# The second attention's twenty column projections: from three 256-column products per eighth to one of 256 and one of 512, with the result in two halves

## The chip, the cores and the metric

The kernel runs on one core of one Trainium2 chip. The metric is the device time of one launch in microseconds (us); the time before is the median of three runs. The engines are named as the profile names them: PE (TensorE's products), PEld (its weight loads), DVE (VectorE), ACT (ScalarE), POOL (GpSimd) and SP (SyncE, which issues most of the transfers).

## What is computed

256 tokens of width 1024 pass through two blocks. The first has a convolution, a gated delta rule, a pooling branch and a layer of 16384 experts. The second block, in which the change lies, is this:

```
h = rmsnorm(x, attn_norm)
proj = h @ w_in                       # 1024 -> 3*512 + 4*512
mq, mk, mv, rq, rk, rv, rg = split(proj)
moba_out = moba_attention(mq, mk, mv)           # 8 heads of 64, causal, ALiBi
ret      = retention_chunkwise(rq, rk, rv)      # 4 heads of 128
ret_out  = head_groupnorm(ret) * silu(rg)
x = x + concat(moba_out, ret_out) @ w_out
... convolved feed-forward layer, gated embedding, last norm
```

The column projections are mq and mk (eight tiles of 128 features, "QK2") and rq, rk, rg (twelve, "RET2"). mv and rv come just before, token by token, as eight weight tiles "V2".

## The kernel before

**Number format.** Every float32 factor is cut into a high and a low part in TensorE's reduced format. A product of x and w is then whi·xhi + whi·xlo + wlo·xhi. For the operand, both parts of an eighth (128 of the 1024 inputs) lie in one buffer, `parts`, of which `ahi` and `alo` are the two slices.

**Weights.** All weights come as tiles of 128x1024 from one array, in the order of their use, through four buffers. Per tile SP issues the transfer, ACT copies it to `whi` (`split_hi`, L454) and DVE subtracts for `wlo` (`split_lo`, L469). `hi_for(u)` and `lo_for(u)` make the tile three ahead of u (u + LEAD); they wait until the tile that had the buffer has been used (`w_used`). The order of the work is written out by hand: each engine has one program, runs it strictly in order, and meets the others at semaphores.

**Projection tiles.** `gemm_tile` (L481) makes 128 features by 256 tokens from one weight tile: eight eighths of three products of 256 columns, 24 products. `gemm_tile_wide` (L491), so far only in the feed-forward layer, needs two per eighth: wlo·xhi of 256 columns, and whi against both parts as one product of 512 columns. Its result lies in two halves of a PSUM bank that have still to be added. In the feed-forward layer ACT copies the upper half to `low` (`ff_low`, L1468) and DVE adds it to the lower one (L2075, L2085).

**Around the change.** PE makes the eight V2 tiles into four banks, then QK2 tile n into one of two banks (`late(4 + n % 2)`), from n = 2 on after result n - 2 has been taken away (`evac2`, L943). DVE takes a result away with one instruction, `scaled` (L1970): times the row of token scales, to `qk2` or `rgs`. After QK2, PE waits for all eight results and begins with `att_scores(0)`. The twelve RET2 tiles alternate between two banks in the same way (L1003), with the heads' attention between them: `att_scores` (waits for `s_max`, which DVE's `att_bias` gives), `att_transposed`, `att_out` (waits for `ao_sb`, which DVE's `att_evac` gives) and `ret_scores`. At the end PE waits for all twenty results (L1013) before the retention's products at L1018. DVE's step n of RET2 is att_bias(n + 1), lo_for, att_norm(n), scaled(n), then att_evac or ret_decay. ACT's program ahead of QK2 is the last `hi_for` of the V2 stretch (L1390), which waits for QK2 tile 0, then the four copies of V2's result to `vv` (L1396), a copy for the embedding (L1399), and the `hi_for` of QK2 (L1400).

Of the kernel before, what the change touches and what calls it, by code (L numbers as in the profile page):

```python
# [19 lines left out]
ALU = mybir.AluOpType  # L20
ACT = mybir.ActivationFunctionType
# [3 lines left out]
T = 256  # L25
# [36 lines left out]
W_QK2 = W_V2 + KT  # L62
N_QK2 = 8
W_RET2 = W_QK2 + N_QK2
N_RET2 = 12
# [6 lines left out]
RING = 4  # L72
# [28 lines left out]
def program(nc, x_tok, vecs, wts, c1, gate_w, rows, w_pool, keys, c2, ple_t, nrows, out):  # L101
    ctx = ExitStack()
    with ctx:
        s = {n: ctx.enter_context(nc.semaphore("s_" + n)) for n in SEMS}
# [5 lines left out]
        def place(name, shape, dt=F32, at=None):  # L110
            size = int(np.prod(shape)) * (2 if dt == F16 else 4)
            size = -(-size // 32) * 32
            if at is None:
                at, top[0] = top[0], top[0] + size
            else:
                at[0], at = at[0] + size, at[0]
            return nc.alloc_sbuf_tensor_at(name, [P] + list(shape), dt, offset=at)
# [136 lines left out]
        qk2 = place("qk2", [16, T], at=a)  # L254
        rgs = place("rgs", [RH, T], at=a)
# [12 lines left out]
        r_row = place("r_row", [T], at=a)  # L268
# [11 lines left out]
        low = place("low", [2, T], at=a)  # L280
        su = place("su", [T], at=a)
        sg = place("sg", [T], at=a)
# [7 lines left out]
        def bank(b0, n, base=0):  # L290

            return flat[:, b0 * 512 + base:b0 * 512 + base + n]

        def late(b0, n, base=0):

            return bank((0, 1, 6, 7, 2, 3, 4, 5)[b0], n, base)
# [181 lines left out]
        def w_k(j, k):  # L478
            return whi[:, j, k * P:(k + 1) * P], wlo[:, j, k * P:(k + 1) * P]

        def gemm_tile(pe, j, dst, content=None):  # L481


            for n in range(KT):
                if content is not None and n % 2 == 0:
                    pe.wait_ge(s["operand"], 4 * content + n // 2 + 1)
                k = 2 * QUARTERS[n // 2] + n % 2 if content == 1 else n
                m = products(dst, *w_k(j, k), ahi[:, k, :], alo[:, k, :], n == 0, n == KT - 1)
            m.then_inc(s["w_used"], 1)

        def gemm_tile_wide(pe, j, dst, content=None):  # L491

            for k in range(KT):
                if content is not None and k % 2 == 0:
                    pe.wait_ge(s["operand"], 4 * content + k // 2 + 1)
                wh, wl = w_k(j, k)
                nc.tensor.matmul(dst[:, 0:T], wl, ahi[:, k, :], start=k == 0, stop=False, skip_group_check=True)  # L497
                m = nc.tensor.matmul(dst, wh, parts[:, :, k, :], start=False, stop=k == KT - 1, skip_group_check=True)  # L498
            m.then_inc(s["w_used"], 1)
# [79 lines left out]
        def _(pe):  # L579
# [342 lines left out]
            for k in range(KT):  # L922
                u = W_V2 + k
# [16 lines left out]
            for n in range(N_QK2):  # L940
                pe.wait_ge(s["w_lo"], W_QK2 + n + 1)
                if n >= 2:
                    pe.wait_ge(s["evac2"], n - 1)  # L943
                gemm_tile(pe, n % RING, late(4 + n % 2, T))


            pe.wait_ge(s["evac2"], N_QK2)
# [51 lines left out]
            for n in range(N_RET2):  # L999
                if n % 2 and n + 1 < MH:  # L1000
                    att_scores((n + 1) // 2)
                pe.wait_ge(s["w_lo"], W_RET2 + n + 1)
                pe.wait_ge(s["evac2"], N_QK2 + n - 1)  # L1003
                gemm_tile(pe, n % RING, late(n % 2, T))
                if n % 2 == 0 and 2 <= n <= MH:
                    att_transposed(n // 2 - 1)
                if n % 2 and 3 <= n <= MH + 1:
                    att_out(n // 2 - 1)
                if n >= MH:
                    ret_scores(n - MH)  # L1010
# [60 lines left out]
            for f in range(FF):  # L1071
                u = W_FF + (3 * f - 1 if f else 0)
# [35 lines left out]
            for k in range(5):  # L1108
                u = W_PLEG + k
# [26 lines left out]
        def _(act):  # L1136
            A = nc.scalar.activation
# [29 lines left out]
            def hi_for(u):  # L1167

                split_hi(act, u + LEAD, (u + LEAD) % 4)
# [227 lines left out]
            m.then_inc(s["v_sb"], 1)  # L1397
            act.wait_ge(s["ple_in"], 16)
            A(pthi[:, :, :], pt[:, :, :], ACT.Copy).then_inc(s["ple_hi"], 1)  # L1399
            for u in range(W_QK2 + 2, W_RET2):  # L1400
                hi_for(u)
            def att_pt(h):
                act.wait_ge(s["pt_ps"], h + 1)
                if h >= 2:
# [3 lines left out]
            def att_exp(h):  # L1408
                act.wait_ge(s["s_max"], h + 1)
                if h >= 4:  # L1410
                    act.wait_ge(s["pt_ps"], h - 3)
                A(pr[:, h % 4, 0:P], sS[:, h % 2, 0:P], ACT.Exp, bias=mx[:, h, 2:3], scale=MD ** -0.5,
                  accum_out=sums[:, h, 0:1])
                A(pr[:, h % 4, P:3 * P], sS[:, h % 2, P:3 * P], ACT.Exp, bias=mx[:, h, 3:4], scale=MD ** -0.5,
                  accum_out=sums[:, h, 1:2]).then_inc(s["s_exp"], 1)

            for n in range(N_RET2):
                u = W_RET2 + n
                hi_for(u)
                if n < MH:  # L1420
                    att_exp(n)
                if n >= 8:
                    act.wait_ge(s["evac2"], N_QK2 + n + 1)
                    A(rgs[:, n - 8, :], rgs[:, n - 8, :], ACT.Silu).then_inc(s["rg_done"], 1)
                if n % 2 == 0 and 2 <= n <= MH:
                    att_pt(n - 2)
                    att_pt(n - 1)
# [47 lines left out]
            for f in range(FF):  # L1475
                u = W_FF + (3 * f - 1 if f else 0)
# [65 lines left out]
        def _(dve):  # L1542
            V = nc.vector
            ch = Chain(dve, s["dve_step"])
# [33 lines left out]
            def lo_for(u):  # L1578
                split_lo(dve, u + LEAD, (u + LEAD) % 4)
# [387 lines left out]
            dve.wait_ge(s["r_bc"], 1)  # L1967
            ch(V.tensor_copy(r_row[:, :], late(7, T)))

            def scaled(u, b0, dst):  # L1970

                dve.wait_ge(s["w_used"], u + 1)
                V.tensor_tensor(dst, late(b0, T), r_row[:, :], ALU.mult).then_inc(s["evac2"], 1)

            for n in range(N_QK2):
                lo_for(W_QK2 + n)
                scaled(W_QK2 + n, 4 + n % 2, qk2[:, n, :])
            dve.wait_ge(s["ple_hi"], 1)
            V.tensor_tensor(ptlo[:, :, :], pt[:, :, :], pthi[:, :, :].bitcast(F32), ALU.subtract).then_inc(s["ple_op"], 1)
            dve.wait_ge(s["c2_in"], 16)  # L1980
# [30 lines left out]
            for n in range(N_RET2):  # L2011
                if n + 1 < MH:
                    att_bias(n + 1)
                lo_for(W_RET2 + n)
                if n < MH:
                    att_norm(n)
                scaled(W_RET2 + n, n % 2, qk2[:, 8 + n, :] if n < 8 else rgs[:, n - 8, :])
                if n % 2 == 0 and 4 <= n <= MH + 2:
                    att_evac(n - 4)
                    att_evac(n - 3)  # L2020
                if n > MH:
                    ret_decay(n - MH - 1)
# [43 lines left out]
            for f in range(FF):  # L2066
                u = W_FF + (3 * f - 1 if f else 0)
                v = f % 2
                lo_for(u)
                dve.wait_ge(s["w_used"], u + 1)  # L2070
                if f >= 2:
                    dve.wait_ge(s["ff_gelu"], f - 1)
                up = su[:, :]
                dve.wait_ge(s["ff_low"], 2 * f + 1)
                V.tensor_tensor(up, late(v, T), low[:, 0, :], ALU.add).then_inc(s["ff_sum"], 1)  # L2075
                dve.wait_ge(s["ff_sum"], 2 * f + 1)
                ch(V.tensor_scalar(fu[:, v, :], up, vcol("conv2", 2 * FF + f), vcol("conv2_b", f), ALU.mult, ALU.add))
                ch(V.scalar_tensor_tensor(fu[:, v, 1:T], up[:, 0:T - 1], vcol("conv2", FF + f), fu[:, v, 1:T],
                                          ALU.mult, ALU.add))
                V.scalar_tensor_tensor(fu[:, v, 2:T], up[:, 0:T - 2], vcol("conv2", f), fu[:, v, 2:T],  # L2080
                                       ALU.mult, ALU.add).then_inc(s["ff_conv"], 1)
                lo_for(u + 1)
                dve.wait_ge(s["w_used"], u + 2)
                dve.wait_ge(s["ff_low"], 2 * f + 2)
                V.tensor_tensor(sg[:, :], late(2 + v, T), low[:, 1, :], ALU.add).then_inc(s["ff_sum"], 1)  # L2085
                dve.wait_ge(s["ff_sum"], 2 * f + 2)
                dve.wait_ge(s["ff_gelu"], f + 1)
                if f >= 2:
                    dve.wait_ge(s["ff_split"], f - 1)
                V.tensor_tensor(pf[:, v, :], fg[:, v, :], sg[:, :], ALU.mult).then_inc(s["ff_mul"], 1)  # L2090
                if f:
                    lo_for(u + 2)
                dve.wait_ge(s["ff_hi"], f + 1)
                V.tensor_tensor(plo[:, v, :], pf[:, v, :], phi[:, v, :].bitcast(F32), ALU.subtract)\
                 .then_inc(s["ff_split"], 1)
# [150 lines left out]
```

## Time and profile before

| | |
|---|---|
| median of three runs | 1301.79 us (1301.33 to 1303.52) |
| the profiled execution | 1304.9 us, of which the span of instructions is 1303.1 us |
| PE busy | 1282.0 us, 98% |
| DVE, ACT busy | 962.9 us (74%), 760.4 us (58%) |
| granted TensorE clock, mean | 0.995 of full speed |

The busy time of PE is the time in which at least one product is recorded as under way. Matmul ends are modelled and products overlap in the records, so the time that a product takes in a stream is the distance from its start to the start of the next one. Times in a timeline are from the start of the span. Brackets at the end of a line give the idle time of the engine before it and what ended that.

### The profile page before, as it was taken

The page shows a single profiled execution, that of the slowest core. Times are in us where ns is not written, and L with a number is a line of the kernel's source. Part 1 is how long each engine was busy: PE and PEld are TensorE (multiplying, and loading weights), DVE is VectorE, ACT ScalarE, POOL GpSimd, SP SyncE. Part 2 cuts the span into 40 slices and gives each one's busy share as a digit, 9 for nine tenths or more (in the row PEclk, how much of TensorE's full clock was granted, in tenths as well). Part 3 has the DMA queues.
Part 4 walks back from the last instruction along what each step waited for, and adds up shares of the span by engine and source line. Part 5 has one row for each costly group of instructions (what it writes and reads, how often), then busy time and mean ns, then how long its engine had stood idle before and what let it go on. Part 6 is the DMA issues. An engine that isn't in the chain of part 4 may idle for free. (4 is left out here: it accounts for less than half of the span.)

```text
span 1303.1 us, 25968 instructions
## 1 busy us (share of the span) xinstructions
PE 1282.0 (98%) x8501; PEld 1165.4 (89%) x8501; DVE 962.9 (74%) x1898; ACT 760.4 (58%) x1153; POOL 484.0 (37%) x276
## 2 busy tenths in 40 slices
PE   8999999999999999998999999999999999999997
PEld 8999899999999999997888888888889988888886
DVE  6886677999899468874666666666666768777775
ACT  6833556777777766654555555555565557555556
POOL 1010001888887888787777674000000000000000
PEclk9999999999999999998999999999999999999999
DMA  7459654767676766667888888777774335555551
GB/s 259 150 179 386 214 178 145 190 182 180 176 193 179 193 178 162 161 161 168 216 216 218 218 215 250 236 240 241 227 247 166 131 131 170 188 190 187 186 193 65
DMA packets 119324, 253.00 MB, mean 194 GB/s; under 512 B 44336, under 2 KB 60848, under 8 KB 118752
## 3 DMA queue, kind: packets, MB, share of 16 engines
q1 hardware_dynamic: 77232, 229.24, 53.9%
q0 software_dynamic: 42032, 22.99, 11.2%
q8 instruction: 33, 0.54, 0.2%
q14 instruction: 27, 0.22, 0.1%
HBM read 234.23 MB, written 17.96 MB: 194 GB/s over the span
## 5 line engine op out<-in xcount | busy, mean ns | idle before, releaser
L469 DVE TENSOR_TENSOR wlo<-raw,whi 128x1024 fp32r<-128x1024 f32 (+1 forms) x500 | 508.5, 1033 | 122.6 <-ACT whi L454 111.4
L454 ACT ACTIVATE whi<-raw 128x1024 fp32r<-128x1024 f32 x412 | 434.8, 1058 | 236.7 <-PE ps L476 225.5
L420 POOL DMA_INDIRECT gates_dense<-gate,spot x256 | 472.5, 1846 | 168.8 <-issue 77.8
L474 PE MATMUL ps<-parts,whi 128*128 128x256 f32 x1472 | 422.4, 287 | 2.1 <-DVE parts L561 1.9
L475 PE MATMUL ps<-parts,whi 128*128 128x256 f32 x1472 | 416.2, 283 | 0.0
L476 PE MATMUL ps<-parts,wlo 128*128 128x256 f32 x1472 | 416.2, 283 | 0.0
L474 PEld LDWEIGHTS ps<-parts,whi 128*128 128x128 f32 x1472 | 282.0, 192 | 4.6 <-issue 4.1
L475 PEld LDWEIGHTS ps<-parts,whi 128*128 128x128 f32 x1472 | 282.1, 192 | 0.0
L476 PEld LDWEIGHTS ps<-parts,wlo 128*128 128x128 f32 x1472 | 281.9, 191 | 0.0
L474 PE MATMUL ps<-whi,phi 128*128 128x512 f32 x600 | 235.3, 392 | 4.9 <-DVE plo L1904 4.3
L475 PE MATMUL ps<-wlo,phi 128*128 128x512 f32 x600 | 234.6, 391 | 0.0
L476 PE MATMUL ps<-whi,plo 128*128 128x512 f32 x600 | 234.5, 391 | 0.0
L474 PEld LDWEIGHTS ps<-whi,phi 128*128 128x128 f32 x600 | 113.3, 189 | 28.8 <-DVE plo L1904 3.8
L1904 DVE TENSOR_TENSOR plo<-ea,phi 128x256 fp32r<-128x256 f32 x128 | 55.1, 430 | 112.4 <-ACT phi L1328 103.4
L476 PEld LDWEIGHTS ps<-whi,plo 128*128 128x128 f32 x600 | 113.3, 189 | 23.9
L475 PEld LDWEIGHTS ps<-wlo,phi 128*128 128x128 f32 x600 | 113.3, 189 | 23.7
L498 PE MATMUL ps<-parts,whi 128*128 128x512 f32 x352 | 125.2, 398 | 0.0
L1317 ACT ACTIVATE ea<-ps 128x256 f32 x116 | 44.5, 384 | 96.6 <-PE ps L476 93.8
L497 PE MATMUL ps<-parts,wlo 128*128 128x256 f32 x352 | 99.1, 282 | 0.9 <-DVE parts L561 0.7
L498 PEld LDWEIGHTS ps<-parts,whi 128*128 128x128 f32 x352 | 66.1, 188 | 16.0
L497 PEld LDWEIGHTS ps<-parts,wlo 128*128 128x128 f32 x352 | 66.4, 189 | 2.5 <-issue 0.9
L438 POOL DMA_DIRECT2D wrow<-in_nrows x1 | 0.6, 580 | 146.7 <-DVE plo L1904 146.7
(373 smaller groups left out, 1320.6 us busy)
## 6 DMA issues: line engine op xcount, KB each, us to landing
raw<-in_wts SPq DMA_DIRECT2D x412, 512.0 KB, 3.9
gates_dense<-pf POOLq DMA_DIRECT2D x4, 4096.0 KB, 30.8
gd<-gates_dense SPq DMA_DIRECT2D x22, 256.0 KB, 5.0
gd<-gates_dense SPq DMA_DIRECT2D x10, 512.0 KB, 6.1
gates_dense<-gate,spot POOLq DMA_INDIRECT x256
cst<-in_c POOLq DMA_DIRECT2D x1, 1216.0 KB, 7.5
xt<-in_x_tok SPq DMA_DIRECT2D x2, 512.0 KB, 4.5
kk<-in_keys POOLq DMA_DIRECT2D x1, 1024.0 KB, 5.2
```

What stands on the lines that cost most here:

```text
L420: pl.indirect_dma_start(out=dense, out_offset=bass.IndirectOffsetOnAxis(ap=spot[:, tb, h, k:k + 1], axis=0), in_=gate[:, tb, h, k:k + 1], ...
L438: pl.dma_start(wrow[:, :, :].rearrange("p a n -> p (a n)"), nrows.partition_broadcast(P)).then_inc(s["nrows_in"], 16)
L454: nc.scalar.activation(whi[:, j, :], raw_tile(j // 2, j % 2), ACT.Copy).then_inc(s["w_hi"], 1)
L469: m = nc.vector.tensor_tensor(wlo[:, j, c], raw_tile(j // 2, j % 2)[:, c], whi[:, j, c].bitcast(F32), ALU.subtract)
L474: nc.tensor.matmul(out_ap, wh, xh, start=first, stop=False, skip_group_check=True)
L475: nc.tensor.matmul(out_ap, wh, xl, start=False, stop=False, skip_group_check=True)
L476: return nc.tensor.matmul(out_ap, wl, xh, start=False, stop=last, skip_group_check=True)
L497: nc.tensor.matmul(dst[:, 0:T], wl, ahi[:, k, :], start=k == 0, stop=False, skip_group_check=True)
L498: m = nc.tensor.matmul(dst, wh, parts[:, :, k, :], start=False, stop=k == KT - 1, skip_group_check=True)
L1317: A(row_of(quad * 4 + n), late(n if four else n % 2, T), ACT.Gelu).then_inc(s["gelu"], 1)
L1904: V.tensor_tensor(plo[:, n % 2, :], row_of(oct_ * 8 + n), phi[:, n % 2, :].bitcast(F32), ALU.subtract)\
```

## The change

All twenty tiles use the wide form into a whole bank. ACT copies the upper half of each result to `low`, which the attention stretch shares with the feed-forward layer. DVE adds the lower half to that copy into `su` or `sg`, waits for the add, and then multiplies by the row of scales as before. ACT's copy of tile n stands in its program after the `hi_for` of step n (in RET2 also after `att_exp(n)`); for QK2 it stands behind the copies to `vv` and for the embedding. The semaphore `ff_low` counts from 20 when the feed-forward layer begins.

```diff
@@ PE, QK2 and RET2
-                gemm_tile(pe, n % RING, late(4 + n % 2, T))
+                gemm_tile_wide(pe, n % RING, late(4 + n % 2, 2 * T))
...
-                gemm_tile(pe, n % RING, late(n % 2, T))
+                gemm_tile_wide(pe, n % RING, late(n % 2, 2 * T))
@@ ACT
             A(pthi[:, :, :], pt[:, :, :], ACT.Copy).then_inc(s["ple_hi"], 1)
-            for u in range(W_QK2 + 2, W_RET2):
-                hi_for(u)
+            def low_half(t, b0):
+                act.wait_ge(s["w_used"], W_QK2 + t + 1)
+                if t >= 2:
+                    act.wait_ge(s["evac2"], t - 1)
+                A(low[:, t % 2, :], late(b0, T, base=T), ACT.Copy).then_inc(s["ff_low"], 1)
+            for n in range(N_QK2):
+                if n >= 2:
+                    hi_for(W_QK2 + n)
+                low_half(n, 4 + n % 2)
...
                 if n < MH:
                     att_exp(n)
+                low_half(N_QK2 + n, n % 2)
@@ DVE
-            def scaled(u, b0, dst):
-                dve.wait_ge(s["w_used"], u + 1)
-                V.tensor_tensor(dst, late(b0, T), r_row[:, :], ALU.mult).then_inc(s["evac2"], 1)
+            def scaled(t, b0, dst):
+                dve.wait_ge(s["ff_low"], t + 1)
+                both = (su, sg)[t % 2][:, :]
+                ch(V.tensor_tensor(both, late(b0, T), low[:, t % 2, :], ALU.add))
+                V.tensor_tensor(dst, both, r_row[:, :], ALU.mult).then_inc(s["evac2"], 1)
...
-                dve.wait_ge(s["ff_low"], 2 * f + 1)
+                dve.wait_ge(s["ff_low"], N_QK2 + N_RET2 + 2 * f + 1)
...
-                dve.wait_ge(s["ff_low"], 2 * f + 2)
+                dve.wait_ge(s["ff_low"], N_QK2 + N_RET2 + 2 * f + 2)
```

## Rows read from the trace of the kernel before

**Rows 1.** Busy time by stretch: stretch, its length, then engines, clock, DMA.
```profile
975.00:999.00 24.00, 23.48 (x196) 23.24 (x194) 13.26 (x17) 11.72 (x14) 0.00 (x0) 1.00 0.54 179
999.00:1047.00 48.00, 48.00 (x410) 44.72 (x411) 38.59 (x92) 26.10 (x58) 0.00 (x0) 1.00 0.40 132
...
1003.00:1027.00 24.00, 24.00 (x210) 22.06 (x210) 22.70 (x62) 13.14 (x35) 0.00 (x0) 1.00 0.41 134
```
**Rows 2.** Timeline of PE (start, us): first products of QK2 tiles 0, 2, 7.
```profile
975.20 0.28 PE L474 MATMUL ps<-parts,whi 128*128 128x256 f32 x1
...
980.95 0.28 PE L474 MATMUL ps<-parts,whi 128*128 128x256 f32 x1
...
995.35 0.28 PE L474 MATMUL ps<-parts,whi 128*128 128x256 f32 x1
```
**Rows 3.** Timeline of PE: two wide feed-forward tiles and what follows them.
```profile
1104.23 0.28 PE L497 MATMUL ps<-parts,wlo 128*128 128x256 f32 x1
...
1107.06 0.28 PE L497 MATMUL ps<-parts,wlo 128*128 128x256 f32 x1
...
1109.88 0.40 PE L474 MATMUL ps<-whi,phi 128*128 128x512 f32 x1
```
**Rows 4.** Timeline of DVE: results of QK2 tiles 0 and 7.
```profile
978.27 0.42 DVE L1973 TENSOR_TENSOR qk<-ps,r_row 128x256 f32<-128x256 f32 x1 [0.44 <-PE ps L476]
...
998.42 0.42 DVE L1973 TENSOR_TENSOR qk<-ps,r_row 128x256 f32<-128x256 f32 x1 [0.49 <-PE ps L476]
```
**Rows 5.** Timeline of PE: the first scores behind QK2, and scores 2.
```profile
998.90 0.49 PE L956 MATMUL ps<-qk 64*128 64x128 f32 x4 [0.52 <-DVE qk L1973]
...
1010.28 0.49 PE L956 MATMUL ps<-qk 64*128 64x128 f32 x4
```
**Rows 6.** Timeline of ACT: the feed-forward layer's copy of an upper half.
```profile
1107.26 0.39 ACT L1473 ACTIVATE low<-ps 128x256 f32<-128x256 f32 x1 [1.70 <-PE ps L498]
```
**Rows 7.** Timeline of DVE: the feed-forward layer's add and its next instruction.
```profile
1107.78 0.42 DVE L2075 TENSOR_TENSOR su<-ps,low 128x256 f32<-128x256 f32 x1 [0.96 <-ACT low L1473]
1108.24 0.41 DVE L2077 TENSOR_SCALAR fu<-su,words 128x256 f32<-128x256 f32 x1
```
**Rows 8.** Timeline of ACT from QK2's tile 0 on.
```profile
978.33 1.06 ACT L454 ACTIVATE whi<-raw 128x1024 fp32r<-128x1024 f32 x1 [1.81 <-PE ps L476]
979.29 2.40 ACT L1396 ACTIVATE vv<-ps,r_col 128x512 f32<-128x512 f32 x4
981.58 0.64 ACT L1399 ACTIVATE pthi<-pt 128x512 fp32r<-128x512 f32 x1
982.10 1.07 ACT L454 ACTIVATE whi<-raw 128x1024 fp32r<-128x1024 f32 x1
```
**Rows 9.** Timeline of DVE: end of bias 3, att_evac 2 and 3, last result.
```profile
1009.35 0.17 DVE L2004 TENSOR_SCALAR mx<-mx 128x2 f32<-128x2 f32 x1
...
1026.97 0.86 DVE L1993 COPY mix<-ps 64x256 f32<-64x256 f32 x2
...
1046.26 0.42 DVE L1973 TENSOR_TENSOR rgs<-ps,r_row 128x256 f32<-128x256 f32 x1 [0.44 <-PE ps L476]
```
**Rows 10.** Timeline of PE: att_out 2, and the retention's first products.
```profile
1030.05 0.44 PE L980 MATMUL ps<-pT,vv 128*64 128x128 f32 x4
...
1046.73 0.49 PE L1018 MATMUL ps<-vv,rS 128*128 128x128 f32 x2
```
**Rows 11.** Timeline of PE: two pauses elsewhere in the kernel.
```profile
8.06 1.95 PE L586 MATMUL ps<-ident,h 128*128 128x128 f32 x16 [1.76 <-ACT h L1156]
...
598.58 0.80 PE L474 MATMUL ps<-whi,phi 128*128 128x512 f32 x1 [3.57 <-DVE plo L1904]
```
**Rows 12.** Busy time by stretch behind the longer pause, and behind the shorter.
```profile
600.00:605.00 5.00, 5.00 (x14) 3.86 (x13) 1.61 (x4) 0.83 (x1) 4.26 (x3) 0.53 0.97 280
605.00:610.00 5.00, 5.00 (x24) 4.14 (x23) 3.16 (x7) 1.90 (x5) 4.21 (x3) 1.00 0.71 176
...
8.00:11.00 3.00, 2.85 (x24) 2.65 (x24) 2.68 (x6) 2.75 (x7) 0.00 (x0) 1.00 0.57 195
```

More of the change, by code:

```diff
@@ L1968, in _ @@
             ch(V.tensor_copy(r_row[:, :], late(7, T)))
-            def scaled(u, b0, dst):
-                dve.wait_ge(s["w_used"], u + 1)
-                V.tensor_tensor(dst, late(b0, T), r_row[:, :], ALU.mult).then_inc(s["evac2"], 1)
+            def scaled(t, b0, dst):
[3 more added lines that the diff above has]
+                V.tensor_tensor(dst, both, r_row[:, :], ALU.mult).then_inc(s["evac2"], 1)
             for n in range(N_QK2):
                 lo_for(W_QK2 + n)
-                scaled(W_QK2 + n, 4 + n % 2, qk2[:, n, :])
+                scaled(n, 4 + n % 2, qk2[:, n, :])
             dve.wait_ge(s["ple_hi"], 1)
@@ L2016, in _ @@
                     att_norm(n)
-                scaled(W_RET2 + n, n % 2, qk2[:, 8 + n, :] if n < 8 else rgs[:, n - 8, :])
+                scaled(N_QK2 + n, n % 2, qk2[:, 8 + n, :] if n < 8 else rgs[:, n - 8, :])
                 if n % 2 == 0 and 4 <= n <= MH + 2:
```

## The prediction

> **What bounds the kernel now.** I read the busy time by stretch first. From 975 us on, where the twenty tiles lie, PE is busy 23.48 of 24.00 us in QK2's stretch and 48.00 of 48.00 in RET2's, at the full granted clock (1.00, the 2.4 GHz level); ACT has about half its time free, DVE between 9 and 11 us in each [rows 1]. So PE is the bound, and only two things count: how long a tile takes on PE, and whether a later evacuation makes PE wait. In the second question an engine's mean load says little. From 1003 to 1027, in the middle of the attention, DVE is busy 22.70 of 24.00 us [rows 1]; it is no bound yet, but has nothing to give away. The timelines of the three engines then show each place at which PE meets ACT or DVE.
>
> **PE's tiles.** Seven narrow tiles lie between the starts at 975.20 and 995.35: 2.88 us each, 24 products at 0.120 [rows 2]. Two wide tiles in a row take 1104.23 to 1107.06 and 1107.06 to 1109.88, 2.825 us each with 16 products [rows 3]. A third fewer instructions thus save 0.054 us a tile, since the columns streamed are the same (6144); over 20 tiles that is -1.1 us, between -1.0 and -1.2 by the two wide tiles shown. Each of the eight products that go per tile is worth 7 ns.
>
> The Trainium skill, "TensorE: Matmul & The Clock Gate", section "Wait — 56ns, not 53.3ns?", gives a fixed cost of about 2.5 ns per product in a warm stream. By that the 160 products that go would be worth 0.4 us (an estimate from that page), and the sum below would end 0.7 us higher; the rows give almost three times as much per product, in this number format, and I go by the rows.
>
> **What an evacuation costs now and then.** Before, DVE's one multiply starts 0.2 us after the tile's end (978.27 against 975.20 + 2.88 = 978.08) and takes 0.42 [rows 2, 4]; PE starts 0.06 after its end (998.84 to 998.90) [rows 4, 5]. After, three steps stand in a row. The nearest rows are those of the same pair in the feed-forward layer: ACT's copy takes 0.39 (1107.26 to 1107.65) [rows 6], DVE's add begins 0.13 later at 1107.78, and the instruction chained to it 0.46 after that, at 1108.24 [rows 7]. So where PE waits for a result without cover, it waits 0.39 + 0.13 + 0.46 = 0.98 us longer. At least the two instructions' own 0.8 us is due; above, 1.1 if each hand-over costs 0.05 more.
>
> **The first tiles of QK2 (the largest term).** There are two banks, so tile 2 needs result 0. ACT's program reaches the copy of half 0 only behind the split that waits for tile 0 (978.33), the four copies to `vv` (979.29, 2.40 us) and the embedding's copy (981.58); its next instruction starts at 982.10 today [rows 8], and 0.05 earlier after, as tile 0 ends 0.05 earlier. From 982.05: copy to 982.44, add at 982.57, multiply 983.03 to 983.45, PE at 983.51. Wide tile 2 could start at 975.20 + 2 x 2.825 = 980.85. PE stands still for 2.7 us. Today the same result leaves at 978.27 [rows 4] and PE runs through (tile 2 at 980.95 [rows 2]): DVE did this alone, and ACT's 2.4 us of V2 copies cost nothing. Without hand-overs it would be 2.3, with DVE's late split in between 3.0. Behind the copy on ACT stand half 1 and the split of the sixth tile, some 0.6 us later than today; PE needs neither before it has done two more tiles, so one stall it is. From tile 3 on the chain of about 1.7 us (0.2 + 0.98 + 0.42 + 0.06) fits into the 2.83 that the other bank gives.
>
> **Behind QK2.** PE waits for all eight results before the first scores, and has nothing else to do: today 0.52 us idle [rows 5]. The full 0.98 comes on top: +1.0 (0.8 to 1.1).
>
> **In the attention.** DVE's add costs its queue 0.46 a tile and nothing leaves it. Two places feel it. First, scores 2 waits for bias 3, which ends at 1009.52 today, 0.70 (with the 0.06) ahead of PE's 1010.28 [rows 5, 9]; two adds make DVE 0.92 later and three wide tiles make PE 0.16 earlier: +0.4 (0.2 to 0.6). Second, att_out 2 waits for DVE's att_evac 2 and 3, done at 1027.83 today, 2.16 ahead of PE's 1030.05 [rows 9, 10]. Seven adds lie before it, 3.22 us; the stretch has 1.30 us idle at most to take them up [rows 1], and part of that is the short gaps of chained instructions, which can't be used. DVE is 1.9 to 3.2 later, PE about level (0.4 later by the first stall, 0.4 earlier by seven tiles): 0 to 1.1, and I take +0.4, as if some 0.6 us of the idle time were usable. ACT, free for nearly half of the time, hides its twenty copies (7.8 us) here: the split behind each copy needs the same tile's end anyway.
>
> **Behind RET2.** The retention's products start at 1046.73, just after the last result (1046.26 + 0.42 = 1046.68) [rows 9, 10]: no cover, +1.0 (0.8 to 1.1). What follows on DVE and ACT moves with PE. The feed-forward layer keeps its instructions, with another count in a wait.
>
> **The sum.** -1.1 + 2.7 + 1.0 + 0.4 + 0.4 + 1.0 = +4.4, with the unrounded terms (-1.07 + 2.66 + 0.98 + 0.38 + 0.40 + 0.98) +4.3 us. The profiled execution (1304.9 us, of which 1303.1 are span) would come to 1309.2 with a span of 1307.4. It lay 3.1 us above the median of the runs; the change does not touch what made that difference, so I add the sum to the median: 1301.8 + 4.3 = 1306.1 us. The low ends together give +2.9 (1304.7), the high ends +5.9 (1307.7).
>
> **Rivals.**
> 1. The front stall doesn't come, only the other terms: +1.6, 1303.4. It takes an ACT that reaches half 0 before 979.4 (980.85 less 0.06, 0.42, 0.46, 0.13 and 0.39). For it: the copy needs nothing that is late. Against it: ACT is strictly in its program's order there, without a gap between 978.33 and 982.10 [rows 8]. 10%.
> 2. Faster: PE's two banks hide every evacuation and its 1.1 us stay: 1300.7. It decides at the same point of ACT and, besides, wherever PE has less than the 0.98 us more of cover at both ends of the tiles. Against it: PE waits there already, 0.52 us before the first scores [rows 5]. 6%.
> 3. The wide form gives nothing beside the attention's small products: -1.1 falls away, +5.4, 1307.2. For it: 0.054 us of 2.88 is near what the rows resolve. Against it: all seven narrow tiles and both wide ones keep their pace [rows 2, 3]. 8%.
> 4. The clock falls in the front stall. After a pause of 3.57 us PE ran at the 1.2 GHz level [rows 11]: in the 5 us from 600 on at 0.53, 14 products of 512 columns instead of the 24 of the next 5 us [rows 12], so 10 x 5/24 = 2.1 us lost there and 0.7 in the 1.4 us before, 2.8 in all. After a pause of 1.76 us, early in the kernel, it read 1.00 [rows 11, 12]. Mine of some 2.5 us lies between. If it falls: +7.1, 1308.9. 12%. The Trainium skill, same page, section "A second HAM failure mode: psum-queue depth-cycling", says that many short idles between groups of products can bring the clock down too; the 0.52 us wait here did not (1.00 in that stretch), and no stall that I add is repeated.
>
> **How the numbers follow.** The forecast as worked out has 64%. The likeliest time is 1306.1. The range leaves out the faster case, most of the clock's case and a few per cent of the ends: 1303.2 to 1308.4. What a measurement of this kernel can tell from no change is about 0.2%, 2.6 us, so slower begins at 1304.4: the forecast (but for 2% at its low end), rivals 3 and 4, together 82%, of which I take 81; within 0.2%: rival 1, that low end and what I held back, 13%; faster 6%.
>
> **What would show it.** In the profile after: L497 and L498 in pairs every 0.353 us in QK2 and RET2; a pause of PE of about 2.4 to 2.7 us before QK2's tile 2, put down to DVE's multiply; ACT's first `low` at about 982, behind the embedding's copy; PE's wait before the first scores 1.5 instead of 0.5; DVE without idle time from 1006 to 1030; a wait of about 1 us before L1018; granted clock 1.00 throughout. The forecast is wrong if tile 2 starts with tile 1's end, if the wide tiles take 2.88 here, or if PE waits in most RET2 tiles for DVE, which would make DVE the bound of that stretch.

## The result and the profile after

The changed kernel takes 1307.26 us (median of 6 runs, 1306.35 to 1310.35) against 1302.50 us for the kernel before in the same job (6 runs, 1301.33 to 1303.52): ratio 1.0044, 95% interval 1.0033 to 1.0054. It is slower, by 4.8 us in the medians.

The profiled executions must be compared by stretch. Their spans are 1304.5 and 1303.1 us, only 1.4 apart, but QK2's tile 0 starts at 972.78 after and at 975.20 before [rows 2], ahead of anything that the change touches. From there to the start of L1025, where the output projection begins, it is 78.26 us after (to 1051.04) and 74.32 before (to 1049.52): **+3.94 us**. The rest, to the end of the span, is 253.5 and 253.6. All stretches below run between these two points.

The busy time by stretch after, in the same columns as [rows 1]; PE is no longer busy throughout, and DVE is busy 23.11 of 24.00 us in the attention:

```profile
975.00:999.00 24.00, 20.47 (x117) 17.51 (x115) 15.22 (x24) 13.04 (x21) 0.00 (x0) 1.00 0.47 159
999.00:1047.00 48.00, 46.62 (x310) 38.74 (x311) 42.37 (x102) 29.27 (x69) 0.00 (x0) 1.00 0.39 133
...
1004.00:1028.00 24.00, 23.57 (x160) 19.54 (x159) 23.11 (x63) 15.25 (x42) 0.00 (x0) 1.00 0.39 133
```

The timeline of ACT after, which answers to [rows 8]: the copies of halves 0 and 1 stand behind V2's four copies and the embedding's, without a gap.

```profile
975.86 1.06 ACT L454 ACTIVATE whi<-raw 128x1024 fp32r<-128x1024 f32 x1 [1.76 <-PE ps L498]
976.83 2.40 ACT L1396 ACTIVATE vv<-ps,r_col 128x512 f32<-128x512 f32 x4
979.10 0.64 ACT L1399 ACTIVATE pthi<-pt 128x512 fp32r<-128x512 f32 x1
979.62 0.67 ACT L1405 ACTIVATE low<-ps 128x256 f32<-128x256 f32 x2
```

The timeline of DVE after: it sat idle for 4.64 us until the half was there, then added and multiplied.

```profile
980.05 0.42 DVE L1984 TENSOR_TENSOR su<-ps,low 128x256 f32<-128x256 f32 x1 [4.64 <-ACT low L1405]
980.51 0.43 DVE L1985 TENSOR_TENSOR qk<-su,r_row 128x256 f32<-128x256 f32 x1
```

The timeline of PE after: the starts of tiles 0 and 1, then the five places where PE waited in the stretch (from 981.08 on, the lines with brackets), three of them with the start of what PE did before. Before, only the first scores had a wait, of 0.52 us [rows 5].

```profile
972.78 0.28 PE L497 MATMUL ps<-parts,wlo 128*128 128x256 f32 x1
...
975.60 0.28 PE L497 MATMUL ps<-parts,wlo 128*128 128x256 f32 x1
...
978.19 0.40 PE L498 MATMUL ps<-parts,whi 128*128 128x512 f32 x1
981.08 0.35 PE L497 MATMUL ps<-parts,wlo 128*128 128x256 f32 x1 [2.50 <-DVE qk L1985]
...
999.36 0.49 PE L956 MATMUL ps<-qk 64*128 64x128 f32 x4 [1.39 <-DVE qk L1985]
...
1009.72 0.82 PE L968 MATMUL ps<-ident,pr 128*128 128x128 f32 x6
1010.97 0.49 PE L956 MATMUL ps<-qk 64*128 64x128 f32 x4 [0.43 <-DVE mx L2016]
...
1027.34 0.36 PE L497 MATMUL ps<-parts,wlo 128*128 128x256 f32 x1
...
1030.94 0.44 PE L980 MATMUL ps<-pT,vv 128*64 128x128 f32 x4 [0.59 <-DVE mix L2005]
...
1047.12 0.39 PE L994 MATMUL ps<-qk 128*128 128x128 f32 x2
1048.25 0.49 PE L1018 MATMUL ps<-vv,rS 128*128 128x128 f32 x2 [0.75 <-DVE rgs L1985]
```

2.50 + 0.87 more than before + 0.43 + 0.59 + 0.75 = 5.14 us of waits. But a bracket counts from the modelled end of the product before it, and in a stream the next product starts ahead of that end: the last one of tile 1 starts at 978.19 and is drawn 0.40 us long, where such products follow each other after 0.23. So the brackets are somewhat short, and the five places are compared by starts here. The lines of the kernel before that answer to L968 and L994, and of run 3 (below) to 1027.34 and 1030.94:

```profile
1009.53 0.81 PE L968 MATMUL ps<-ident,pr 128*128 128x128 f32 x6
...
1046.48 0.38 PE L994 MATMUL ps<-qk 128*128 128x128 f32 x2
```
```profile
1021.48 0.36 PE L497 MATMUL ps<-parts,wlo 128*128 128x256 f32 x1
...
1024.43 0.44 PE L980 MATMUL ps<-pT,vv 128*64 128x128 f32 x4
```

Tile 2 starts 5.48 us after tile 1 instead of 2.825 [rows 3], 2.65 late. The first scores are 0.87 late (1.39 less 0.52). Scores 2 start 1.25 us after L968's first product instead of 0.75 (1010.28 [rows 5]), 0.50 late; att_out 2 starts 3.60 us after its tile instead of 2.95, 0.65 late; the retention's products start 1.13 us after L994 instead of 0.25 (1046.73 [rows 10]), 0.88 late. That is 5.55 us; the stretch grew by 3.94, so the products gave back 1.6.

### The profile page after: what moved, and what is told of

It is laid out like the page before. It is cut to its first block and busy times, and to the rows that moved or that the text cites. A ratio compares the mean times of both kernels' runs of the same rounds, so it can differ in the third digit from the quotient of the medians.

```text
span 1304.5 us, 25706 instructions
## 1 busy us (share of the span) xinstructions
PE 1279.7 (98%) x8341; PEld 1155.6 (89%) x8341; DVE 971.2 (74%) x1918; ACT 766.2 (59%) x1173; POOL 483.5 (37%) x276
## 5 line engine op out<-in xcount | busy, mean ns | idle before, releaser
L474 PE MATMUL ps<-parts,whi 128*128 128x256 f32 x1312 | 376.2, 287 | 1.9 <-DVE parts L561 1.8
L475 PE MATMUL ps<-parts,whi 128*128 128x256 f32 x1312 | 371.0, 283 | 0.0
L474 PEld LDWEIGHTS ps<-parts,whi 128*128 128x128 f32 x1312 | 251.4, 192 | 2.6 <-issue 2.2
L475 PEld LDWEIGHTS ps<-parts,whi 128*128 128x128 f32 x1312 | 251.5, 192 | 0.0
L498 PE MATMUL ps<-parts,whi 128*128 128x512 f32 x512 | 181.5, 396 | 0.0
L498 PEld LDWEIGHTS ps<-parts,whi 128*128 128x128 f32 x512 | 96.1, 188 | 22.3
L1483 ACT ACTIVATE low<-ps 128x256 f32<-128x256 f32 x44 | 16.9, 384 | 64.6 <-PE ps L498 64.5
```

Source lines behind the costliest of these rows:

```text
L474: nc.tensor.matmul(out_ap, wh, xh, start=first, stop=False, skip_group_check=True)
L475: nc.tensor.matmul(out_ap, wh, xl, start=False, stop=False, skip_group_check=True)
L1483: A(low[:, n, :], late(2 * n + f % 2, T, base=T), ACT.Copy).then_inc(s["ff_low"], 1)
```

## Experiments

The theory: all cost lies in the later evacuation of results, at five places, and the products themselves save about 1.1 us. The rivals: the products or the clock cost the time; or a wait that is taken away only moves to the next place. Line numbers are each kernel's own.

**1. The changed kernel again**, as a base.

> The changed kernel once more, as the base of this job. Theory (the late evacuations: 5.1 us of waits in the trace after, less 1.1 us that the products save): +4 to +5 us against the kernel before. Second question: two of its six runs so far lay 3 us above the others, with a lower mean clock (0.994 and 0.995 against 0.996 and 0.997). Rival for the part of the loss that the one trace does not hold: the 2.5 us pause ahead of QK2's tile 2 lets the clock fall in some executions. Then runs 3 us above the lowest show up here again and are gone in the run without that pause.

1305.05 us (1304.09 to 1306.18) against 1301.51 (22 runs, 1300.50 to 1302.99): ratio 1.0031, interval 1.0019 to 1.0043. The stretch is 78.23 us, with the same five waits (2.50, 1.39, 0.43, 0.54, 0.75). No run lies 3 us above the others here, so the two high ones of the first job did not come again; their cause stays open, as no trace shows them. The spread of 2 us is that of the kernel before; the last section shows a difference of this size that arises ahead of QK2.

**2. ACT's order at the front.** The definition of `low_half` moves ahead of the first line shown.

```diff
...
+            low_half(0, 4)
             act.wait_ge(s["w_used"], W_QK2)
             act.wait_ge(s["scale_ok"], 1)
             for b0 in range(4):
+                if b0 == 3:
+                    low_half(1, 5)
                 m = A(half_row(vv, b0), late(b0, 512), ACT.Copy, ...)
...
                 if n >= 2:
                     hi_for(W_QK2 + n)
-                low_half(n, 4 + n % 2)
+                    low_half(n, 4 + n % 2)
```

> ACT copies half 0 ahead of the four V2 copies and half 1 ahead of the last of them; nothing else differs from the changed kernel. Theory: the 2.5 us pause ahead of tile 2 goes, the other four waits stay: 2.5 us faster than the changed kernel, +1.5 to +2.3 against the kernel before. Rival A (DVE's longer queue is what counts, and the pause only moves): the waits at the first scores grow by what is gained, within 1 us of the changed kernel. Rival B (the clock falls in that pause in some executions): besides the 2.5 us, the spread between the lowest and the highest run shrinks from 4 us to about 2, as it was before the change.

1303.51 us (11 runs, 1301.79 to 1304.04): 1.0012, interval 1.0003 to 1.0021. The stretch falls to 75.83 us, 2.4 less than in run 1 on the same chip, and the other four waits stand as they were. PE's waits in this kernel (total, times, longest):

```profile
PE ps L956 <- DVE qk L1989: 1.4, 1, 1.4
PE ps L1018 <- DVE rgs L1989: 0.8, 1, 0.8
PE ps L980 <- DVE mix L2009: 0.6, 1, 0.6
PE ps L956 <- DVE mx L2020: 0.4, 1, 0.4
```

So the order of ACT's program makes the largest term. Rival A falls. Rival B is not borne out: the spread is 2.3 us with the pause gone, and was 2.1 in run 1.

**3. The products alone.** The kernel before with `gemm_tile_wide` at both places and nothing else; the upper half of each result is left out.

> The kernel before with the wide products alone: ACT copies nothing and DVE multiplies the lower half as before, so the products of the low part of the operand are left out of the result. Theory: all cost of the change is in taking the results away; this is 1.1 us faster than before (0.054 us a tile), and QK2's tiles start every 2.825 us without a pause. Rival (the wide form gives nothing here, or its stream is held up by the attention's products): no change or slower.

1299.24 us (11 runs, 1298.73 to 1301.46): 0.9986, interval 0.9977 to 0.9995. The stretch is 72.90 us, 1.42 less than before. PE has one wait left, the old one:

```profile
PE ps L956 <- DVE qk L1973: 0.5, 1, 0.5
```

QK2's tiles start 2.82 to 2.84 us apart instead of 2.88, as forecast; up to the first scores that is 0.41 us (23.70 to 23.29). RET2's gain more, 1.01 us or 0.08 a tile: from the start of its tile 1 to that of tile 2 it is 2.89 instead of 2.98, from tile 8 to tile 9 (with other products between) 4.11 instead of 4.21.

**4. The evacuation alone.** The changed kernel with `gemm_tile` at both places, and `late(b0, T)` in ACT's copy.

> The changed kernel with the narrow products of before; ACT copies the lower half instead of an upper one, so DVE's add doubles the result. Theory: it has all five waits and none of the saving: +5 us against before, 1.1 us slower than the changed kernel; the pause ahead of tile 2 is 0.1 us shorter, as two narrow tiles take 0.1 longer. Rival (the products cost the time, not the evacuation): near the kernel before.

1307.09 us (5 runs, 1305.70 to 1308.02): 1.0045, interval 1.0032 to 1.0059. The stretch is 80.46 us, +6.14, more than the +5 expected. The profile shows four waits (2.44, 0.87 more than before, 0.16 and 0.74) and none at att_out 2; by starts the five places are 2.60, 0.88, 0.23, 0.20 and 0.87 late, 4.8 us, less than in the changed kernel. The rest is the clock: the pause is no longer than in run 1, but behind it PE ran at the 1.2 GHz level for about three us. The busy time by stretch, with the clock in the last column but two:

```profile
977.00:979.00 2.00, 0.20 (x2) 0.00 (x0) 0.39 (x1) 2.00 (x6) 0.00 (x0) 1.00 0.04 14
979.00:982.00 3.00, 2.36 (x11) 2.39 (x12) 2.93 (x6) 0.80 (x1) 0.00 (x0) 0.51 0.08 18
982.00:985.00 3.00, 3.00 (x25) 3.00 (x25) 1.06 (x3) 0.95 (x2) 0.00 (x0) 0.92 0.82 287
```

Tile 2 takes 4.21 us here instead of 2.88: 1.33 us for the clock, and 4.8 + 1.3 = 6.1. In run 1 the same place reads 1.00:

```profile
976.00:979.00 3.00, 0.51 (x4) 0.21 (x2) 1.02 (x3) 3.00 (x6) 0.00 (x0) 1.00 0.11 45
979.00:982.00 3.00, 3.00 (x18) 2.67 (x19) 2.86 (x4) 0.14 (x1) 0.00 (x0) 1.00 0.25 86
```

**5 and 6. One stage at a time.** Tiles outside the set are narrow and are taken away by the old single multiply.

```diff
+        WIDE = (8, ..., 19)        # run 5: RET2's; run 6: (0, ..., 7), QK2's
...
+                if t not in WIDE:
+                    dve.wait_ge(s["w_used"], W_QK2 + t + 1)
+                    V.tensor_tensor(dst, late(b0, T), r_row[:, :], ALU.mult).then_inc(s["evac2"], 1)
+                    return
```

> Only RET2's twelve tiles are wide and taken away in halves; QK2's eight are as before. Theory (each wait belongs to its own tiles): the waits of the trace after at scores 2, att_out 2 and the retention's products stay (0.4 + 0.6 + 0.8), the two at QK2 go, the products give back 0.7 to 1.0: +0.8 to +1.1 us against before in the stretch. Rival (DVE's lag in the attention comes from what QK2 left behind): the attention's waits vanish too, and it is no slower than before.

RET2 alone: 1302.45 us (12 runs) against 1302.09 (32 runs), ratio 1.0003, interval 0.9994 to 1.0012. The stretch is 75.37 us, +1.05, with waits of 0.43, 0.58 and 0.75 and the old 0.52: as expected.

> Only QK2's eight tiles are wide; RET2 is as before. Theory: the pause of 2.5 us ahead of tile 2 and 0.9 more at the first scores, less 0.4 for the products: +2.9 us, and some 1.2 more where the clock falls in the pause, as it did in the trace of the run with the evacuation alone. With the RET2 part alone it adds up to the changed kernel's +4. Rival (the two parts hide each other): the two sums differ from the changed kernel by more than 1 us.

QK2 alone: 1306.97 us (9 runs, 1303.76 to 1308.18), ratio 1.0031, interval 1.0020 to 1.0043. The stretch is 78.64 us, +4.32, of which the clock is about 1.5 again: behind the pause of 2.50 us it is at 0.52, and tile 2 takes 4.31 us instead of 2.8.

```profile
978.00:981.00 3.00, 0.88 (x5) 0.50 (x3) 0.62 (x2) 3.00 (x7) 0.00 (x0) 1.00 0.24 90
981.00:984.00 3.00, 2.62 (x8) 2.34 (x9) 2.97 (x5) 0.54 (x1) 0.00 (x0) 0.52 0.17 40
```

Without it, 1.05 + 2.8 = 3.9 us: in the traces the two stages add up to the changed kernel's 3.94, and neither hides the other. The medians don't show that: QK2 alone is 4.9 us above the kernel before there, more than the whole change in run 1 (3.5). Its two quickest runs (1303.76 and 1304.49 us) have the highest mean clock, 0.998; the other seven have 0.995 or 0.996, in which the falls near 597 us (last section) count too.

**7. Front order, last tiles narrow.** Experiment 2 with tiles 7 and 19 narrow (`WIDE` = 0 to 6 and 8 to 18).

> ACT copies halves 0 and 1 ahead of the V2 copies, and the last tile of QK2 and of RET2 are narrow and taken away in one step, as before. Theory: only DVE's two waits in the attention are left (0.4 + 0.6) against 18 tiles' saving (1.3): -0.3 us against before, no measurable change. Rival (a wait that is filled moves to the next place): the first scores or the retention's products wait as long as in the changed kernel, +1.6 as without the front pause alone.

1302.57 us (12 runs, 1300.44 to 1305.45), ratio 1.0003, interval 0.9994 to 1.0013: no difference from before. The stretch is 74.53, +0.21 where -0.3 was expected; DVE's two waits are left (0.42, 0.54), and 0.21 before the retention's products. By starts the three places are 0.48, 0.60 and 0.35 late, 1.4 us, against the saving of 18 tiles (about 1.3): +0.1 of the +0.21. The forecast left out the last place: DVE's weight split behind tile 18's two instructions ends only at 1043.9, and the multiply of tile 19 follows it without idle time, where before DVE stood idle for 0.44 us ahead of it [rows 9].

**8. POOL multiplies.** As run 7; for RET2's tiles 0 to 7 DVE only adds.

```diff
+            for t in range(N_QK2, N_QK2 + 8):                      # POOL
+                pl.wait_ge(s["zero_ok"], t - N_QK2 + 2)
+                pl.wait_ge(s["evac2"], t)
+                nc.gpsimd.tensor_tensor(qk2[:, t, :], (su, sg)[t % 2][:, :], r_row[:, :], ALU.mult).then_inc(s["evac2"], 1)
...
+                if N_QK2 <= t < N_QK2 + 8:                         # DVE, in scaled
+                    dve.wait_ge(s["evac2"], t - 1)
+                    V.tensor_tensor(both, late(b0, T), low[:, t % 2, :], ALU.add).then_inc(s["zero_ok"], 1)
+                    return
...
```

`zero_ok` is a semaphore that an earlier part of the kernel has left at 1; here it counts DVE's adds.

> As the run before this one, but for RET2's first eight tiles POOL, idle there, multiplies by the row of scales, and DVE only adds. Theory (DVE's queue is what makes the attention wait): DVE has the load of before, both waits go and the products' saving stays: -1.2 us against before. Rival (POOL's multiply, which no trace here shows, is slow or holds DVE up): DVE's instructions or the results are later than before, and the waits at scores 2 and att_out 2 stay or grow.

1301.08 us (12 runs, 1299.26 to 1301.80), ratio 0.9991, interval 0.9983 to 1.0000. The stretch is 73.08 us, -1.24 where -1.2 was expected; 0.25 of that is a faster pace of QK2's tiles 2 to 6 in this execution (2.77 us, last section), which run 11 doesn't have. POOL takes 0.74 us for what takes DVE 0.42, and both waits in the attention are gone. POOL's timeline, then PE's waits:

```profile
1003.26 0.74 POOL L444 TENSOR_TENSOR qk<-sg,r_row 128x256 f32<-128x256 f32 x1 [2.70 <-DVE sg L2007]
```
```profile
PE ps L966 <- DVE qk L2001: 0.5, 1, 0.5
PE ps L1029 <- DVE rgs L2001: 0.2, 1, 0.2
```

So it was the extra instruction in DVE's queue that made the attention wait. Beside POOL, DVE's copies to `mix` (0.86 us) and its bias instructions (0.55) take as long as elsewhere. One weight split overlaps a multiply of POOL, and takes 1.63 us; the others in the stretch take 1.22 or 1.23. The two lines:

```profile
1025.77 1.63 DVE L473 TENSOR_TENSOR wlo<-raw,whi 128x1024 fp32r<-128x1024 f32 x1 [0.27 <-ACT whi L458]
```
```profile
1025.59 0.73 POOL L444 TENSOR_TENSOR qk<-sg,r_row 128x256 f32<-128x256 f32 x1 [2.94 <-DVE sg L2007]
```

It is the same in run 11: the split beside POOL's last multiply takes 1.63 us, the others 1.22 or 1.23.

**9. The pause filled.** The changed kernel; PE makes seven products of ones in the pause.

```diff
+                if n == 2:
+                    spin(7, late(6, P))
                 if n >= 2:
                     pe.wait_ge(s["evac2"], n - 1)
```

> The changed kernel, in which PE makes seven products of ones into a free bank in the pause ahead of QK2's tile 2, so that it is not idle there for 2.5 us. In the traces so far the clock fell behind that pause in two of four (the run with the evacuation alone, and QK2 alone), at 1.3 to 1.5 us. Theory (it falls for want of products in the pause): the granted clock stays 1.00 from tile 0 to the first scores, the other waits are as in the changed kernel, and the stretch takes 78.2 us in each execution: +3.9 against before. Rival (the fall has another cause): the profile shows it here too.

1306.00 us (5 runs, 1305.66 to 1306.77) against 1301.51 (15 runs): 1.0038, interval 1.0024 to 1.0051. The stretch is 78.17 us at 1.00 throughout; the fill took 1.72 us and left 0.84 idle. That agrees with the theory, but one trace can't tell it from an execution in which the clock would have stayed up anyway, and the ratio is no lower than run 1's. Inconclusive as to the cause.

**10. The pause longer.** The changed kernel with `hi_for(W_QK2 + 2)` ahead of `low_half(0, 4)`.

> The changed kernel, in which ACT makes one more split (1.06 us) ahead of half 0. Theory: the pause ahead of tile 2 is 1.0 us longer, 3.5 us, and the clock falls behind it in nearly every execution, as behind the 3.57 us of rows 11: +1.0 for the pause and 1.3 to 2.8 for the clock, +6.2 to +7.7 against before. Rival (the clock's fall does not hang on the length of the pause): the pause and 1.0 us alone, +4.9.

1308.03 us (5 runs, 1305.95 to 1308.42): 1.0048, interval 1.0034 to 1.0061. The pause is 3.44 us, the stretch 82.12: +3.9 against run 1, 1.0 for the pause, 2.7 for the clock (tiles 2 and 3 take 5.25 and 3.10 us) and 0.2 for the pace of the tiles behind (2.82 us, not 2.77).

```profile
975.00:979.00 4.00, 1.67 (x10) 1.17 (x8) 0.00 (x0) 4.00 (x9) 0.00 (x0) 1.00 0.35 125
979.00:980.00 1.00, 0.00 (x0) 0.00 (x0) 0.88 (x3) 0.33 (x2) 0.00 (x0) 0.57 0.00 0
980.00:985.00 5.00, 4.88 (x16) 4.24 (x17) 3.00 (x4) 0.00 (x0) 0.00 (x0) 0.50 0.44 158
```

Four of its five runs lie within 0.5 us of 1308.2; the fifth, at 1305.95, has the highest mean clock (0.998). A pause 1.0 us longer lost about twice as much to the clock as in runs 4 and 6; that it falls in nearly every execution is likely, but only the profiled one shows it.

**11. Run 8 again**, on another chip.

> The kernel with POOL's multiply, front order and narrow last tiles once more, as its interval against before ended at 1.0000. Theory: 1.2 us less in the stretch, ratio 0.999. Rival (its gain was the spread of an earlier pause that all kernels have, around 597 us): ratio 1.000, with the stretch as long as before (74.3 us).

1299.72 us (11 runs) against 1301.51 (15 runs): 0.9991 again, interval 0.9982 to 1.0000; the stretch is 73.36 us, -0.96: the saving of 18 tiles (1.3) less 0.35 before the retention's products. It is the fastest complete version, by about 0.1% of the kernel before. Each interval ends at 1.0000, so the runs alone barely show it; the shorter stretch in both traces is the stronger sign.

## Why the prediction was right

It said 1306.1 us and +4.3; the runs gave +4.8 and +3.5 in their medians, the stretch of the two traces +3.94. The direction and the five places were as forecast. By starts the terms came out as -1.6, +2.65, +0.87, +0.50, +0.65 and +0.88, where the forecast had -1.1, +2.7, +1.0, +0.4, +0.4 and +1.0. That the sum was only 0.4 too high is partly luck: the saving and the hand-overs were better than forecast by 0.75 us, the attention's waits worse by 0.37.

- **PE's tiles**: -1.1 forecast, -1.42 measured with the products alone. QK2's 0.055 a tile was read rightly; RET2's 0.08 was not to be seen in a stream without other products between. Another 0.2 of the 1.6 in the trace after is the pace of the tiles behind the front pause (2.77 us, last section). Per product that goes the 1.42 are 8.9 ns (1.42 / 160), in QK2 alone 6.4 (0.41 / 64). Both lie well above the 2.5 ns that the Trainium skill gives ("TensorE: Matmul & The Clock Gate", section "Wait — 56ns, not 53.3ns?").
- **Front**: 2.66 forecast, 2.65 measured by starts: tile 2 starts 8.30 us after tile 0 (972.78 to 981.08), and 8.31 was forecast (975.20 to 983.51). Here two small errors cancelled, DVE's add 0.09 sooner and PE 0.08 later than assumed. 2.4 came back with ACT's order; without the pause the tiles behind it run at 2.82 again, which makes the difference. The row of ACT in program order was enough to see it. The low bound of 2.3 was a slip: without its hand-overs (0.13, 0.04 and 0.06) the forecast's own rows give 2.4.
- **First scores and retention's products**: +1.0 each; +0.87 and +0.88 (0.75 by its bracket). From the start of ACT's copy to DVE's add it is 0.43 us at the front (979.62 to 980.05), not 0.52; these 0.1 us are what both places lack.
- **Attention**: +0.4 and +0.4; 0.43 and 0.59 by the brackets. For the second, the end of DVE's att_evac 3 after:

```profile
1029.93 0.87 DVE L2005 COPY mix<-ps 64x256 f32<-64x256 f32 x2
```

  From the first scores to there it is 28.93 us before (998.90 to 1027.83) and 31.44 after (999.36 to 1030.80), 2.5 later where seven adds are 3.2. So some 0.7 us of DVE's idle time were usable; the 0.6 assumed was read well. The forecast's rows gave 3.22 - 0.6 - 2.16 = 0.46, rounded down to 0.4. The other 0.13 is PE's side: it started 0.14 us after DVE's end instead of 0.06, and without its wait would have been there after 30.99 us instead of 31.15, although it had waited 0.43 at scores 2, as RET2's tiles gave back more than forecast.
- **The clock** was underrated. I put it between a pause that didn't lower it (1.76) and one that did (3.57), at 12%. It fell behind pauses of 2.44 and 2.50 us in two traces (runs 4 and 6) and not behind 2.50 in two others (after and run 1), at 1.3 to 1.5 us rather than the 2.8 taken from the longer pause. It belongs into the forecast as a share of the executions, not as a separate case. How large that share is in the changed kernel's runs was not settled, and so it stays open what part of the 4.8 us in the first medians it makes.

## What to carry to other kernels

A cheaper product that needs one more engine to take its result away is paid at each place where the consumer has no cover: the first tile that reuses a bank, and every "wait for all results". Look at what stands ahead of the new instruction in that engine's program, not at its mean load; moving two instructions gave back 2.4 of 3.9 us. Compare pauses of PE by the starts of its products; the idle time of the profile can be 0.1 us or more short at each of them. Where a queue is nearly full, half a microsecond per tile shows up later, at a wait on other work of that queue.

## What the runs showed of the hardware that was not expected

All kernels here, the one before too, have a pause of PE near 597 us, and what the clock does behind it differs between executions. In run 1 it is 1.79 us and the clock stays at 1.00; after, 2.22 us, and the next 5 us are at 0.85; before, 3.57 us [rows 11]. From the after trace:

```profile
597.37 0.50 PE L474 MATMUL ps<-whi,phi 128*128 128x512 f32 x1 [2.22 <-DVE plo L1914]
```
```profile
595.00:600.00 5.00, 2.78 (x10) 2.11 (x9) 5.00 (x9) 1.63 (x3) 4.39 (x3) 0.81 0.72 164
600.00:605.00 5.00, 5.00 (x20) 4.05 (x19) 1.92 (x5) 1.54 (x3) 4.08 (x4) 0.85 1.05 292
```

A pause of 1.87 us (run 6) went with a fall and one of 2.07 us (run 5) without (0.91 and 1.00 from 590 to 610), so the length alone does not decide in this range. QK2's tile 0 starts between 970.6 and 971.3 us in the seven traces at 1.00 there, between 972.4 and 973.1 in the five at 0.91, and at 975.20 in the profile of before, at 0.83. The first two groups lie as far apart as the runs of each kernel spread, some 2 us, and the profile of before lies 3 us above its median; that the runs' spread comes from here fits that, but was not tested.

Behind the front pause, QK2's wide tiles start every 2.77 us (after, runs 1, 6 and 9) and not every 2.82, as without it (runs 2, 3, 7 and 11) and behind the longest pause (run 10). But the pause isn't needed: in run 8, which has none, tiles 2 to 6 start every 2.77 us too, and run 11 is the same kernel. What makes the difference was not found out.
